# Two transformer blocks on one core: the split weight tiles moved by 64 bytes in their partitions, the tiles behind them by 128

## The reference

```
for each of three layers:
    h = rms_norm(x, pre);  m = mixer(h);           x = x + rms_norm(m, post)
    h = rms_norm(x, pre2); f = (silu(h @ w_gate) * (h @ w_up)) @ w_down
    x = x + rms_norm(f, post2)
```

## The kernel before, in words

| tile | first byte | remainder by 128 | by 512 |
|---|---|---|---|
| `w_hi` | 44032 | 0 | 0 |
| `w_lo` | 66560 | 0 | 0 |
| `h_hi` | 105408 | 64 | 448 |
| `h_lo` | 121792 | 64 | 448 |
| `g_hi` | 138176 | 64 | 448 |
| `g_lo` | 183232 | 64 | 448 |
| `nsa_out` | 154560 | 64 | 448 |
| `fox_parts` | 173056 | 0 | 0 |

## Time and profile before

### The profile page before, as it was taken

The page is one execution under the profiler, slowest core; times in us unless marked ns, Lnnn a source line. Parts: engine busy times, 40 slices in busy tenths (PEclk is TensorE's granted clock), DMA queues, the critical chain, the costliest instruction groups (busy, mean ns, idle before and its releaser), DMA issues.

```text
span 1897.1 us, 25590 instructions
## 1 busy us (share of the span) xinstructions
PE 1861.5 (98%) x9410; PEld 1510.6 (80%) x9410; DVE 811.3 (43%) x1365; ACT 430.2 (23%) x880; POOL 1239.9 (65%) x743
## 2 busy tenths in 40 slices
PE   9999999999999999999999999999999999999997
PEld 7886678888888898777888888889778888888886
DVE  6355755433331144254543333015984453334103
ACT  4336663111110021131311111003334221111000
POOL 7975537866666657664876667557665686666652
PEclk9999999999999999999999999999999999999998
DMA  6431002333333214212233333222323233323311
GB/s 208 132 114 46 12 1 78 110 90 93 95 113 107 79 45 158 83 49 67 89 100 100 88 101 116 100 71 67 100 67 90 78 100 89 99 89 110 106 61 45
DMA packets 44877, 168.27 MB, mean 89 GB/s; under 512 B 4984, under 2 KB 7288, under 8 KB 44672
## 3 DMA queue, kind: packets, MB, share of 16 engines
q1 hardware_dynamic: 44496, 164.56, 27.9%
q10 hardware_dynamic: 304, 2.64, 0.4%
HBM read 165.07 MB, written 2.11 MB: 88 GB/s over the span
## 4 chain that ended last, share of the span: by engine, by line
PE 91%; DVE 4%; POOL 3%; issue 1%; ACT 1%; DMA 0%; POOLq 0%; SPq 0%; DVEq 0%
PE psum L583 27%; PE psum L585 27%; PE psum L584 27%; PE psum L801 2%; POOL w_lo L470 1%; PE psum L785 1%; DVE h_lo L1556 1%; DVE tmp L1598 1%; PE psum L827 1%; POOL w_hi L467 1%; PE psum L633 1%; PE psum L824 1%; PE psum L917 1%; PE psum L931 1%; POOL x L491 1%
## 5 line engine op out<-in xcount | busy, mean ns | idle before, releaser
L470 POOL TENSOR_TENSOR w_lo<-raw,w_hi 128x1024 fp32r<-128x1024 f32 (+1 forms) x286 | 748.4, 2617 | 23.8
L583 PE MATMUL psum<-h_hi,w_hi 128*128 128x512 f32 (+1 forms) x1744 | 663.8, 381 | 13.4 <-POOL w_lo L470 7.4
L584 PE MATMUL psum<-h_lo,w_hi 128*128 128x512 f32 (+1 forms) x1744 | 657.0, 377 | 0.0
L585 PE MATMUL psum<-h_hi,w_lo 128*128 128x512 f32 (+1 forms) x1744 | 657.0, 377 | 0.0
L467 POOL TENSOR_SCALAR w_hi<-raw 128x1024 fp32r<-128x1024 f32 (+1 forms) x286 | 323.7, 1132 | 472.5 <-PE psum L585 446.6
L583 PEld LDWEIGHTS psum<-h_hi,w_hi 128*128 128x128 f32 x1744 | 327.6, 188 | 90.3 <-issue 15.9
L585 PEld LDWEIGHTS psum<-h_hi,w_lo 128*128 128x128 f32 x1744 | 327.2, 188 | 67.7
L584 PEld LDWEIGHTS psum<-h_lo,w_hi 128*128 128x128 f32 x1744 | 327.3, 188 | 66.1 <-issue 0.2
L583 PE MATMUL psum<-g_hi,w_hi 128*128 128x512 f32 (+1 forms) x594 | 219.1, 369 | 0.0
L584 PE MATMUL psum<-g_lo,w_hi 128*128 128x512 f32 (+1 forms) x594 | 218.5, 368 | 0.0
L585 PE MATMUL psum<-g_hi,w_lo 128*128 128x512 f32 (+1 forms) x594 | 218.5, 368 | 0.0
(11 more groups left out here) (282 smaller groups left out, 1876.4 us busy)
## 6 DMA issues: line engine op xcount, KB each, us to landing
raw<-in_wide SPq DMA_DIRECT2D x239, 512.0 KB, 3.6
raw<-in_down SPq DMA_DIRECT2D x48, 704.0 KB, 4.0
decay<-decay_rows ACTq DMA_DIRECT2D x1, 2048.0 KB, 7.8
out<-x SPq DMA_DIRECT2D x16, 128.0 KB, 1.7
x<-in_xt SPq DMA_DIRECT2D x3, 512.0 KB, 6.9
x<-in_xt ACTq DMA_DIRECT2D x1, 512.0 KB, 4.6
angles<-in_angles SPq DMA_DIRECT2D x1, 512.0 KB, 10.4
cols<-in_cols SPq DMA_DIRECT2D x1, 221.0 KB, 4.4
```

The lines of the kernel that those rows point to most:

```text
L470: nc.gpsimd.tensor_tensor(w_lo[:, slot, 0:w], raw[:, j % RAW, 0:w], w_hi[:, slot, 0:w].bitcast(F32), ALU.subtract).then_inc(units_split, 1)
L583: pe.matmul(out_ap, lhs[0], rhs[0], start=first, stop=False)
L584: pe.matmul(out_ap, lhs[0], rhs[1], start=False, stop=False)
L585: return pe.matmul(out_ap, lhs[1], rhs[0], start=False, stop=last)
```

## The change

A tile of 16 float32 (64 bytes in each partition) that nothing uses is allocated in front of `w_hi`, and another behind `w_lo`. So `w_hi` and `w_lo` lie 64 bytes further on, and everything allocated after them 128 bytes further. `x`, `cols`, `tabs`, `ones` and `raw` stay. No instruction is added or removed. The remainder by 128 changes for the weights alone (0 to 64); by 512 `w_hi` and `w_lo` come to 64, the `h`, `g` and `nsa_out` tiles from 448 to 64, `fox_parts` from 0 to 128.

```diff
         raw = sb("raw", [P, RAW, DOWN_UNIT * P])
+        sb("in_front_of_w", [P, 16])
         w_hi = sb("w_hi", [P, SLOTS, DOWN_UNIT * P], F32R)
         w_lo = sb("w_lo", [P, SLOTS, DOWN_UNIT * P], F32R)
+        sb("behind_w", [P, 16])
         squares = sb("squares", [P, 2, S])
```

## The result

The changed kernel takes 1871.53 us (median of 4 runs, 1869.28 to 1873.12), the kernel before 1900.09 us in the same comparison. The ratio is 0.9849 with a 95% interval of 0.9832 to 0.9866: 28.6 us, or 1.5%, faster. Foretold were 1869.0 us. The profiled execution took 1873.12 us, its span 1870.9 us.

What follows compares the result with a forecast made beforehand. PE was taken to bound the kernel, with 91% of the chain, through the distance between dense matmuls. The terms summed to -30.3 us, from 1899.3 to 1869.0 us, with a range of 1860 to 1914.

Steps and rivals of the forecast that it cites:

- the lower bound: Dense triples of 512 columns: after the change a triple costs 680 ns, as with fox_parts, against an upper bound of some 707.
- the relation: Dense matmuls: the difference between moving and stationary places sets the distance, so equal remainders are faster, near 1869 us; chance 0.48.
- two readers at once: Dense matmuls: the next weight load reads while the matmul streams its moving tile, a natural cause for their places mattering.
- The objection that it raised: Places (64, 0) and (0, 64) cost differently, so the relation by 128 can't be all; by 512 they are -64 and +64.
- 512 columns, `h` and `g`: 1766 dense triples that PE paces, 1304 with h and 462 with g, at -20 ns each: -35.3 us.
- 512 columns, weights moving: 64 triples with moving weights on stationary h, from some 687 to 680 ns: -0.4 us.
- 512 columns, `fox_parts`: 28 triples with moving fox_parts, losing what the others win, +20 ns each: +0.6 us.
- halves of 256 columns, `h` and `g`: Triples of 256 columns go to 360 ns: +20 ns for some 175 and +7 for some 190, +4.8 us.
- the 88 woven triples: Triples with h between attention steps, 11 units of 8, left out of the gain because a faster PE would wait longer.
- What was costed at nothing: DMAs, ACT, DVE and POOL at the new places, including POOL writing the weights, which waits 1.75 us for PE: no cost.
- the moving tile's own place decides: Rival for the dense triples: the stationary place has no effect, only moving weights lose, +0.8 us, result 1900.1; chance 0.25.
- each place pays for itself: Rival for the dense triples: 7 ns for the stationary and 20 for the moving tile, (64, 64) at 707, 1913.2 us; chance 0.27.

Runs made afterwards that it cites:

- three kernels that run at 680 ns: The changed kernel, 1871.53 us; against the kernel before, only 64 bytes behind the weights, 1871.66 us, and only 320 bytes behind them, 1872.89 us.
- h_lo_alone: Against the kernel before, h_lo alone moved, to 0 by 256, with h_hi, g_hi, g_lo and the weights left in place: 1903.70 us, ratio 1.0017.
- w_lo_alone: Against the kernel before, w_lo alone moved to 448 by 512, w_hi at 0, all other tiles keeping their remainder: 1896.64 us, ratio 0.9982.
- the mixed kernels: Kernels with one tile at another offset: w_lo alone 1896.64 us, h_lo alone 1903.70 us, w_lo at +64 with the rest at 0 1891.47 us.

## Why the prediction was right

**The step that carried it.** The prediction took the lower bound for the triples of 512 columns, because equal remainders were the case of `fox_parts`. It holds: 680 ns, to the nanosecond. The choice between the bounds was a narrow one (0.48 for the relation), and its reason, two readers at once, no run has shown; what the experiments show is the relation itself. There was luck in the change too: it brings `h` and `g` to offset 0 by 128, by 256 and by 512 alike, so the prediction did not have to know which of them counts. The objection that it raised, that -64 and +64 differ and so 128 can't be the whole rule, was the right one. 256 is the number, and both its signs stay apart: 700 at -64, 687 at +64.

**The terms.** I took the distances from each matmul's start to the next, by kind, in both traces. For a kind of `three` the term is the change of the mean of its distances under 0.26 us, which hold no wait, times their number: with `h` moving 233.3 to 227.1 ns over 4342 distances, with `g` 233.3 to 226.7 over 1386. The last row is what is left of the difference of the two spans.

| term | foretold us | traces us |
|---|---|---|
| 512 columns, `h` and `g` | -35.3 | -36.3 (`h` -27.1, `g` -9.2) |
| 512 columns, weights moving | -0.4 | -0.4 |
| 512 columns, `fox_parts` | +0.6 | +0.1 |
| halves of 256 columns, `h` and `g` | +4.8 | +4.4 |
| everything else, waits and attention work | 0 | +6.0 |
| together | -30.3 | -26.2 |

The dense term is a little larger, since some triples between attention steps and in the openings gain as well. `fox_parts` was priced at +20 ns a triple and lost 7: the prediction let it lose what the others win, as if its offset became -64, and it became +64. The spans are those of the two profiled executions, and the changed one was the slowest of its four runs; between the medians the gain is 28.6 us.

The last row was left out of the sum. 5.4 us of it are in the distances behind small products outside `three`, those of the attention and of the norms. The largest piece, 2.5 us, is clock. In the norm of the Conformer PE runs 48 products of one column. Eight of them take 0.90 us from start to start at the clock of 2.4 GHz and 1.71 us at that of 1.2 GHz, as these rows show, of the kernel before first and then of the changed one:

```profile
1450.96 1.03 PE L1135 MATMUL psum<-ones,y_dw 128*128 128x1 f32 x8
1451.86 1.17 PE L1135 MATMUL psum<-ones,squares 128*128 128x1 f32 x8
```

```profile
1432.48 1.84 PE L1137 MATMUL psum<-ones,y_dw 128*128 128x1 f32 x8
1434.19 1.84 PE L1137 MATMUL psum<-ones,squares 128*128 128x1 f32 x8
```

In the kernel before the clock fell at the last two of the 48, in the changed kernel 24 products earlier, and it stayed low for 10 us rather than 7. The windows around the norm say the same (columns as in the earlier trace rows, the clock is the last but two):

```profile
1440.00:1490.00 50.00, 49.75 (x230) 40.50 (x229) 23.41 (x40) 18.66 (x28) 23.47 (x14) 0.93 0.25 74
```

```profile
1420.00:1470.00 50.00, 49.18 (x222) 41.08 (x222) 22.52 (x39) 18.57 (x27) 21.56 (x14) 0.90 0.20 64
```

PE was busy right up to the fall in both, with triples and then with these small products. All three kernels that run at 680 ns show 0.90 there. Of the other nine all but two show 0.93; `h_lo_alone`, at 703 ns a triple, shows 0.90 too and `w_lo_alone` 0.97. The mean clock of whole runs says it more broadly: 0.988 to 0.991 in the 10 runs of those three kernels, 0.990 to 0.994 in the runs of the kernel before, means 0.989 and 0.992. So the gain in the matmuls was partly given back in clock. Why the clock falls earlier is not settled by these runs. The other 3.5 us of the row are small pieces of both signs, mostly in the mixers, where the prediction assumed for the 88 woven triples that PE gains and then waits; they are not attributed.

**The halves.** They went to 360 ns, as `fox_parts` had shown them. The prediction gave them their own price, and with it a sign against the main term. This was right, and 210 of the 272 with `h` and 110 of the 132 with `g` take exactly that. At -64 a half takes 340 or 353 ns and keeps it for a stretch: with the same tiles the opening of the last feed-forward part ran at 340 for 10 us and then at 353, and that of the first mostly at 353. What chooses between them, no run shows. Of such a pair shows one each. The groups of the changed kernel have lost the difference between `h` and `g`:

```profile
L585 PE MATMUL psum<-h_hi,w_hi 128*128 128x256 f32 x272 | 78.6, 289 | 3.1 <-DVE h_lo L1558 3.1
L585 PE MATMUL psum<-g_hi,w_hi 128*128 128x256 f32 x132 | 37.8, 286 | 0.0
```

**What was costed at nothing.** POOL writes the weights at their new place in the same time. Its busy time went from 1239.9 to 1237.7 us, and the time in which it waited before L467 fell from 472.5 us to 446.3 over 286 instructions, 0.09 us each. The wait in the middle of the 286 fell from 1.75 to 1.59 us, by the 0.16 that the prediction gave a unit of the feed-forward part. There it still waits for PE, as two in a row of the changed kernel show (1.75):

```profile
985.34 1.05 POOL L469 TENSOR_SCALAR w_hi<-raw 128x1024 fp32r<-128x1024 f32 x1 [1.59 <-PE psum L587]
...
990.78 1.05 POOL L469 TENSOR_SCALAR w_hi<-raw 128x1024 fp32r<-128x1024 f32 x1 [1.92 <-PE psum L587]
```

**The rivals.** That the moving tile's own place decides falls with the kernel that has only the bytes in front: `h` at 0 there, and 700 ns. That each place pays for itself falls with (64, 64) at 680. The Trainium skill's rule of two independent ports ("TensorE: Matmul & The Clock Gate", Part 2) says that loading the next weights steals no read bandwidth of SBUF from the running matmul. By that rule alone no place would matter, and these runs differ from it: a stationary tile is read by its loads alone, and moving it by 64 bytes against a moving tile that stays put changes the triple by 20 ns in 700 (bytes in front against bytes behind). What in the memory they share, the runs do not show. That it is the load beside the matmul and not another one is argued, not shown: the records of one triple's distances in the mixed kernels did not single one out.

## What to carry to other kernels

When TensorE is busy all the time, look at the distance from one matmul's start to the next and compare kinds that differ only in where their tiles lie; two kinds with different distances are a free measurement of placement. To tell a tile's own place from a relation of two, move each of them alone. In a stream of float32-rounded matmuls with 512 columns, put stationary and moving tiles at the same byte by 256 in their partitions, all of them: in this kernel 64 bytes of unused space were worth 1.5%. Mixing offsets within a stream can cost more than leaving all of them at a bad one. And check the narrower matmuls apart, as they may want another offset.

## What was not expected of the hardware

- The distance depends on the offset by 256 bytes and not smoothly: 680 ns a triple at 0, 687 at +64, 690 to 706 at +128 and -128, 700 in the mean at -64, 698 to 703 at +32 and -32.
- The stream keeps a pattern once it has one. At -16 the same instructions on the same tiles run at 700 ns for a long while and then at 680; halves at -64 keep 340 or 353. With `w_lo` alone at 0 one feed-forward part runs at 697 to 703 and two at 693 or 694. These two kernels also scatter most, over 11 and nearly 12 us between runs; the changed kernel's runs lie within 4 us.
- Two matmuls of three at a worse offset did not cost two thirds of the difference: with `h_lo` alone at offset 0, a triple took some 703 ns, more than the 700 with none there.
